# Shorter steps for the first attention, its head norms among the projections, and four smaller edits at the ends of stages

## The reference, cut to what matters

```
q = rms_norm(q.reshape(B, L, N_Q_HEADS, HEAD_DIM), q_norm_g)      # 8 heads of 64
k = rms_norm(k.reshape(B, L, N_KV_HEADS, HEAD_DIM), k_norm_g)     # 2 heads of 64
p = softmax(concatenate([s_band, s_meta, sink], axis=-1))         # window 128, block 128
out = p[band] @ v + p[meta] @ v_meta
...
mixed = concatenate([rms_norm(attn), rms_norm(ssm)]); h = h + mixed @ w_out
h = h + peer_ffn(rms_norm(h, norm2_g), ...)                       # 128 tiles of U, 128 of V
# second model, two layers:
x = x + 0.5 * swiglu(rmsnorm(x), w_gate, w_up, w_down)            # ffn1
x = x + (four mixers of rmsnorm(x)) @ w_out
x = x + 0.5 * swiglu(rmsnorm(x), w_gate, w_up, w_down)            # ffn2
```

## Time and profile before

| What | Value |
| --- | --- |
| median of 3 runs | 4655.22 us (4654.63 to 4656.16) |
| the profiled execution | 4656.73 us, span 4655.5 us |
| PE busy | 4155.0 us, 89% |
| DVE busy | 2403.9 us, 52% |
| ACT busy | 1352.5 us, 29% |
| POOL busy | 110.0 us, 2% |
| granted clock, mean | 0.922 |
| split on DVE (L343), mean of one | 1232 ns |
| projections of the first block end, first step of the merged part begins | 111.3 us |
| merged part ends, w_out begins | 373.6 us |

### The profile page before, as it was taken

The page is one execution under the profiler, slowest core; times in us unless marked ns, Lnnn a source line. Parts: engine busy times, 40 slices in busy tenths (PEclk is TensorE's granted clock), DMA queues, the critical chain, the costliest instruction groups (busy, mean ns, idle before and its releaser), DMA issues.

```text
span 4655.5 us, 46825 instructions
## 1 busy us (share of the span) xinstructions
PE 4155.0 (89%) x19069; PEld 3256.1 (70%) x19069; DVE 2403.9 (52%) x3798; ACT 1352.5 (29%) x2068; POOL 110.0 (2%) x210
## 2 busy tenths in 40 slices
PE   7468999999999999998998756899999987479999
PEld 6357887666678888877877535787778775357877
DVE  4834898777734444443323876433233249763331
ACT  3143322333333333323222222322132232223221
POOL 7000000000000000000000000000000000000000
PEclk9678999999999999999999776899999998768999
DMA  3002354555566666642332110123222221101231
GB/s 104 0 10 64 99 144 136 157 180 181 181 197 192 184 193 188 188 143 89 95 95 73 41 52 1 55 92 98 91 77 95 95 64 46 47 1 64 91 99 68
DMA packets 253334, 473.52 MB, mean 102 GB/s; under 512 B 15856, under 2 KB 138896, under 8 KB 250944
## 3 DMA queue, kind: packets, MB, share of 16 engines
q1 hardware_dynamic: 253120, 470.53, 33.1%
HBM read 399.95 MB, written 70.52 MB: 101 GB/s over the span
## 4 chain that ended last, share of the span: by engine, by line
PE 77%; DVE 17%; ACT 4%; issue 1%; DMA 0%; POOL 0%; DVEq 0%; ACTq 0%; POOLq 0%; SPq 0%
PE ps L352 23%; PE ps L353 22%; PE ps L354 22%; PE ps L455 2%; DVE arena L1792 2%; DVE arena L2642 1%; DVE st L2640 1%; PE ps L2191 1%; PE ps L2167 1%; DVE arena L2559 1%; DVE wtwo L343 1%; DVE arena L1108 1%; DVE arena L1788 1%; DVE arena L1789 1%; PE ps L1641 1%
## 5 line engine op out<-in xcount | busy, mean ns | idle before, releaser
L343 DVE TENSOR_TENSOR wtwo<-wraw,wtwo 128x1024 fp32r<-128x1024 f32 x414 | 508.5, 1232 | 832.4 <-ACT wtwo L333 832.1
L352 PE MATMUL ps<-XH,wtwo 128*128 128x512 f32 (+1 forms) x1936 | 794.5, 410 | 1.3 <-DVE XL L481 1.3
L353 PE MATMUL ps<-XL,wtwo 128*128 128x512 f32 (+1 forms) x1936 | 764.2, 395 | 0.0
L354 PE MATMUL ps<-XH,wtwo 128*128 128x512 f32 (+1 forms) x1936 | 761.2, 393 | 0.0
L333 ACT ACTIVATE wtwo<-wraw 128x1024 fp32r<-128x1024 f32 x414 | 435.5, 1056 | 447.0 <-PE ps L354 433.9
L343 DVE TENSOR_TENSOR wlast<-wraw,wlast 128x1024 fp32r<-128x1024 f32 x204 | 250.2, 1228 | 433.0 <-ACT wlast L333 432.9
L354 PEld LDWEIGHTS ps<-XH,wtwo 128*128 128x128 f32 x1936 | 365.6, 189 | 87.2
L352 PEld LDWEIGHTS ps<-XH,wtwo 128*128 128x128 f32 x1936 | 366.5, 189 | 74.6 <-issue 2.2
L353 PEld LDWEIGHTS ps<-XL,wtwo 128*128 128x128 f32 x1936 | 367.2, 190 | 70.9
L352 PE MATMUL ps<-XH,wlast 128*128 128x512 f32 x912 | 378.4, 415 | 4.5 <-DVE wlast L343 4.5
L354 PE MATMUL ps<-XH,wlast 128*128 128x512 f32 x912 | 362.4, 397 | 0.0
(11 more groups left out here) (445 smaller groups left out, 6742.1 us busy)
## 6 DMA issues: line engine op xcount, KB each, us to landing
wraw<-in_ut SPq DMA_DIRECT2D x128, 512.0 KB, 4.2
wraw<-in_v SPq DMA_DIRECT2D x128, 512.0 KB, 3.9
wraw<-in_ffn_gate SPq DMA_DIRECT2D x88, 512.0 KB, 3.5
wraw<-in_ffn_up SPq DMA_DIRECT2D x88, 512.0 KB, 3.5
wraw<-in_ffn_down SPq DMA_DIRECT2D x88, 512.0 KB, 3.6
acts<-arena SPq DMA_DIRECT2D x128, 256.0 KB, 4.5
gates<-arena SPq DMA_DIRECT2D x16, 2048.0 KB, 9.0
arena<-gates SPq DMA_DIRECT2D x32, 1024.0 KB, 8.1
```

The lines of the kernel that those rows point to most:

```text
L343: ve.e.tensor_tensor(W.items[n][8], W.rawof(n), W.items[n][7], ALU.subtract).then_inc(*ve.up("wlo", n))
L352: mm(out, lh, rh, start=start, stop=False)
L353: mm(out, lh, rl, start=False, stop=False)
L354: return mm(out, ll, rh, start=False, stop=stop)
```

## The change

Six edits:

1. **Units in four steps.** A unit's steps are now: scores of unit n + 1; turns of heads 0 and 1 and the value product of head 0; the rest of the turns and products; one step without PE work. ACT makes all four copies of a unit (L811), in the second and third step, and the exponentials of unit n + 1 come behind them, in the fourth. DVE makes no copies. The turned probabilities have one PSUM bank (3), the products another (4); before there were two banks for the turns and half of bank 2 for the products. The attention has 39 steps, the SSM still 60.
2. **Head norms among the projections.** DVE's work for q's heads stands behind the copies of q, and ACT's square root behind the splits for k and v; k's heads are done among the u projections.
3. **`xD` by token tile**: PE waits for each diagonal ahead of its matmul, in all eight norms.
4. **`ac_table`**: a square root of one column, put at the end of the attention's half of `ac_out`, ahead of the splits of `w_out` in both mixers, ahead of the splits of the down tiles in all four networks, and ahead of the first `ac_prep` of the V phase. It makes the compiler load the Sqrt table there.
5. **`TAIL` = 18**: the last four down tiles of each network are taken token tile by token tile, and DVE waits for each bank by itself. They form a group, so their places come back together.
6. **Waits** for `coef` and `masks` stand once, ahead of the units.

```diff
         for j in range(8):
             o = k.open(0, 8, "xT", n, j)
-            pe.wait_ge(*at("xD", n))
             for i in range(4):
+                pe.wait_ge(*at("xD", n, i))
...
+def ac_table(k):
+    k.ac.after().activation(k.ssq[:, 7:8], k.ones[:, 0:1], ACT.Sqrt).then_inc(*k.ac.up())
...
-        na, ns = 6 + 3 + 7 * 8 + 5 + 1 + 5, 60
+        na, ns = 3 + 8 * 4 + 4, 60
...
         splits(k, split_ac, "kv", 256)
+        self.ac_heads("q", 0, 32)
...
+        q = self.ve_heads(self.Q, "Q", 8, 4, 0, "q")
+        next(q)
         for c in range(2):
             split_ve(k, ("kv", c))
+        next(q)
...
+        kn = self.ve_heads(self.KV[:, :, 0:128], "KV", 2, 5, 40, "k")
         for m in range(4):
             split_ve(k, ("u", m))
+            if m < 2:
+                next(kn)
...
+            def turn(hq):
+                pe.wait_ge(*at("se", n))
+                o = k.open(3, 4, "pT", n, hq)
+                ...
+            def value(h):
+                pv = k.open(4, 5, "pv", n) if h == 0 else k.got("pv", n)
+                pe.wait_ge(*at("PT", n, h))
+                ...
+            yield
+            if n < 7:
+                scores(n + 1)
+            yield
+            turn(0)
+            turn(1)
+            value(0)
+            yield
+            turn(2)
+            value(1)
+            turn(3)
+            value(2)
+            value(3)
+            yield
...
         for n in range(8):
-            lo = 0 if n // 2 else 128
-            ...
+            yield
+            yield
+            turned(n, 0)
+            turned(n, 1)
+            yield
+            turned(n, 2)
+            turned(n, 3)
+            yield
             if n < 7:
-                yield from front(n + 1)
+                exps(n + 1)
...
     def ac_v(self):
         k, ac, at = self.k, self.k.ac, self.k.at
+        ac_table(k)
         for j in range(self.LEAD):
             self.ac_prep(j)
...
+        ws = {f: k.W.pair((*id, "down", f)) for f in range(self.TAIL, 22)}
+        for m in range(4):
+            for f, w in ws.items():
+                pe.wait_ge(*at("wlo", w[2]))
+                for n in range(2):
+                    last = one(f, m, n, w)
+                    if f == 21:
+                        last.then_inc(*pe.up("down", *id, "tile", m, n))
...
-        ve.wait_ge(*at("down", *id, 21))
         for m in range(4):
             for n in range(2):
+                ve.wait_ge(*at("down", *id, "tile", m, n))
```

More of the change, by code:

```diff
@@ L693, in ve_in, with ac_heads, ve_heads @@
         k.end("in", ve)
+    def ac_heads(self, name, base, n):
+        k, ac = self.k, self.k.ac
+        ac.wait_ge(*k.at(name + "var"))
+        ac.e.activation(k.st[:, base:base + n], k.st[:, base:base + n], ACT.Sqrt).then_inc(*ac.up(name + "sd"))
+    def ve_heads(self, x, event, nh, n, base, name):
+        k, ve, v, at = self.k, self.k.ve, self.k.ve.e, self.k.at
+        x = x.rearrange("p i (h e) -> p i h e", e=64)
+        t4 = self.tmp[:, 0:n * nh * 64].rearrange("p (i h e) -> p i h e", h=nh, e=64)
+        ss = k.st[:, base:base + n * nh]
+        for i in range(n):
+            ve.wait_ge(*at(event, i))
+        ve.after().tensor_tensor(t4, x, x, ALU.mult).then_inc(*ve.up())
+        ve.after().tensor_reduce(ss.rearrange("p (a b) -> p a b", b=nh), t4, AX, ALU.add).then_inc(*ve.up())
+        ve_rstd1(k, ss, 64).then_inc(*ve.up(name + "var"))
+        yield
+        ve.wait_ge(*at(name + "sd"))
+        v.reciprocal(ss, ss).then_inc(*ve.up())
+        ve.after().tensor_tensor(x, x, bc(ss.rearrange("p (a b) -> p a b", b=nh), 3, 64),
+                                 ALU.mult).then_inc(*ve.up(name + "n"))
+        yield
     def blocks(self, i):
@@ L713, in pe_att, with scores @@
         pe.e.transpose(o[:, 0:128], KV[:, 4, 0:128], k.ident[:, :]).then_inc(*pe.up("kT"))
-        yield
-        yield
-        def front(n):
+        def scores(n):
             i, hh = n // 2, n % 2
@@ L735, in front @@
                 last.then_inc(*pe.up(f"sm{r // 64}", n))
[L736 to L740, removed]
+        yield
+        scores(0)
         for n in range(8):
             i, hh = n // 2, n % 2
-            if n < 7:
-                yield from front(n + 1)
             vals = [None if kb == 0 and i == 0 else KV[:, (i - 1, i, 4)[kb], 128 + 64 * hh:192 + 64 * hh]
                     for kb in range(3)]
[L747 to L766, removed]
@@ L777, in ac_att, with exps @@
         a = ac.e.activation
+        st = k.st
         k.begin(ac, "in", "pe", "ac", "ve")
[L779 to L788, removed]
+        def exps(n):
             i = n // 2
@@ L798, in front, with turned @@
             last.then_inc(*ac.up("se", n))
-            yield
-        yield from front(0)
-        for n in range(8):
-            lo = 0 if n // 2 else 128
-            if n < 7:
[L805 to L815, removed]
+        def turned(n, hq):
+            lo = 0 if n // 2 else 128
+            ac.wait_ge(*at("pT", n, hq))
+            if 4 * n + hq >= 3:
+                ac.wait_ge(*at("pv", (4 * n + hq - 3) // 4, (4 * n + hq - 3) % 4))
+            a(self.PT[(4 * n + hq) % 3][:, lo:384], k.got("pT", n, hq)[:, lo:384],
+              ACT.Copy).then_inc(*ac.free(("pT", n, hq)))
+            ac.note("PT", n, hq)
+        yield
+        yield
+        exps(0)
+        for n in range(8):
+            yield
+            yield
+            turned(n, 0)
+            turned(n, 1)
+            yield
+            turned(n, 2)
+            turned(n, 3)
+            yield
+            if n < 7:
+                exps(n + 1)
+        yield
         ac.wait_ge(*at("ao", 7))
@@ L867, in ve_att, with largest @@
         last.then_inc(*ve.up())
-        yield
         sk = k.row("sink")
         ve.wait_ge(*at("rows"))
-        def front(n):
-            yield
+        ve.wait_ge(*at("masks"))
+        def largest(n):
             i, hh = n // 2, n % 2
@@ L883, in front @@
             ve.wait_ge(*at("sm1", n))
-            ve.wait_ge(*at("masks"))
             if n >= 2:
@@ L894, in front @@
             ve.after().tensor_scalar(mx, mx, -1.0, None, ALU.mult).then_inc(*ve.up("smx", n))
+        yield
+        largest(0)
+        for n in range(8):
+            i, hh = n // 2, n % 2
+            s0 = 64 + 16 * (n % 2)
+            den, es = st[:, s0 + 4:s0 + 8], st[:, s0 + 8:s0 + 12]
             yield
+            yield
+            if n < 7:
+                largest(n + 1)
             yield
@@ L1966, in plan_ffn @@
     for f in range(22):
-        k.W.add((name, l, "down", f), k.d[f"{name}_down{l}"][128 * f:128 * f + 128, :], 1, 1024)
+        k.W.add((name, l, "down", f), k.d[f"{name}_down{l}"][128 * f:128 * f + 128, :], 1, 1024,
+                group=(name, l, "tail") if f >= Ffn.TAIL else None)
 class Ffn:
+    TAIL = 18
     def __init__(self, k, name, l, gname, norm, last, before):
```

124 lines of the change are left out of this document (59 added, 65 removed).

## The result

The changed kernel takes 4577.72 us (median of four runs, 4575.17 to 4580.67) against 4655.69 us before (four runs, 4654.63 to 4657.46): a ratio of 0.9832, with a 95% interval from 0.9815 to 0.9849. That is 78 us less, where 70 were forecast. Its profiled execution took 4580.15 us, with a span of 4578.9 us against 4655.5; the mean granted clock rose from 0.922 to 0.929. Its four runs lie in two pairs, two near 4575.2 and two near 4580.4, and the profiled one is of the upper pair; so a difference of up to 3 us to the median is within their own spread.

The account below looks back on a forecast made before the run. PE carries 77% of the chain of waits; gains lie where it stands still, merged part and seams. 35 + 16.5 + 7.5 + 6.1 + 5 = 70 us less: 4585 us median; likeliest case 4572 to 4600, overall range 4562 to 4612.

Parts of the forecast that it names:

- (a): Merged part's start: moving head norms among the projections saves 11.3 us, less 0.5 for slowing POOL (at most 3).
- (b): Merged part's first stretch, to the SSM's 17th step: 3.5 units instead of 1.3 make it 21 us longer (13 to 30).
- (c): DVE's long stretch of 14 steps: 3.5 units instead of 2, fewer copies, 5 us longer (3 to 10).
- (d): The y stretch, 76.1 us: three units and the Exp/Gelu switches leave, 22 us less (12 to 32).
- (e): GLU to the SSM's end, 42.1 us: scores, a value product and exponentials with their table load leave, some 5 us less.
- (h): Diagonals: PE starts behind the first of four, 0.94 us less in each of eight norms, 7.5 us.
- (f): End of the merged part: the 23.4 us in which only the attention's rest runs go whole.
- (g): Down tiles: 4.1 us less behind three networks, 4.2 at the fourth; 16.5 us in sum (13 to 17).
- (i): Tables: six norms lose their load, 7.7 us less; the V phase adds 1.6 us; net 6.1 us.
- (j): Clock: shorter waits give 1 us in each of six norms, V's start may lose 1; net 5 us less.
- the first rival: Merged part gives only the head norms back: it gains 15 us, the change 50, giving 4605 us; chance 0.17.
- everything overlaps better: Clock stays high and y stretch falls: 46 us from merged part, 16 clock, 30 rest, giving 4563 us; chance 0.12.

Follow-up runs that it names:

- e7: Changed kernel with the V phase's table fetch moved from ahead of its first tile to behind its ninth: 4576.58 us, ratio 0.9830 to before.
- e6: Changed kernel with POOL's scratch and the head norms' scratch exchanged, so q's scalings overwrite nothing POOL reads: 4572.43 us, ratio 0.9820 to before.
- e1: Kernel before with only the last four down tiles of each network taken token tile by token tile: 4641.29 us, ratio 0.9964.
- e4: Kernel before with only the merged part's edits (units in four steps, copies on ACT, head norms among the projections): 4610.83 us, ratio 0.9898.
- e2: Kernel before with only one event for each of a norm's four diagonals: 4650.64 us, ratio 0.9987.
- e3: Kernel before with only the square root's table fetched early in four places: 4659.65 us, ratio 1.0003.
- e10: Changed kernel without the four early table fetches: 4587.68 us, ratio 0.9853 to before.
- e8: Changed kernel with two banks in turn for the turned probabilities, values' products back in the scores' third bank: 4578.14 us, ratio 0.9836 to before.
- e5: Changed kernel with the head norms of q and k back at the beginning of the merged part: 4586.95 us, ratio 0.9852 to before.
- e9: Kernel before with all seam edits together (down tiles, diagonals, tables), merged part as it was: 4626.11 us, ratio 0.9936.
- e11: Changed kernel with both the exchanged scratch of e6 and the later V table fetch of e7: 4573.18 us, ratio 0.9824 to before.
- e12: e11 plus 24 identity products filling PE's wait ahead of each norm but the first: 4579.55 us, ratio 0.9837 to the kernel before.

## Why the prediction was right, and where its terms were off

The time and its direction came as forecast, within the likeliest case's own range. The terms, in their order:

(a) Wrong in its small part, right in its large one. The head norms' 11.3 us went, but POOL's slowing cost 2.9 to 4.5 us of wait (e7's and the changed kernel's rows) instead of 0.5. A single split beside POOL was the wrong row to size it by. The sum of DVE's two-operand operations, 6.4 us, was the right measure, and my upper bound of 3 us was too low. e6 took this loss away.

(b), (c), (d), (e) The stretches last 54.5, 74.1, 52.1 and 35.3 us, forecast 57, 75, 54 and 37. Each was a little shorter, and the part started 3.1 us earlier, of which (h) had only 0.94; e1, which changes nothing ahead of it, starts it 2.4 us earlier too, so some 2 us are the spread of the projections. The merged part's term was therefore too small: 35 forecast, 41.7 in the profiled execution, 45.6 in e4, whose y stretch had the higher clock. The mechanism is the one named: units in PE's idle time, copies no longer behind long operations (PE's wait ahead of the value products, 67.5 us, is 11.7), and the 23.4 us of (f) gone whole. No run takes the four steps and the copies on ACT apart, so their shares are argued from the rows.

(g) 16.5 forecast, 15.2 in e1. The waits fell to 5.4 us there (5.6 expected). With (h) and (i) the waits ahead of norms 1 to 7 should have lost 26.6 us, and lost 27.7.

(h) 7.5 forecast, 5.8 in e2: of 0.94 us less wait a norm keeps part, as the half clock then reaches further into its matmuls (4.5 us of wait leave 2.5 us lost in norm 7, 5.4 us left 2.1).

(i) Its mechanism held: no load in seven of the eight norms, a load of 1.28 us at the V phase. Its size can't be told by itself: −3 in e3, +10 in e10. By the Trainium skill ("ScalarE: Activation LUTs", What ACT_TABLE_LOAD costs) a switch has a drain of 1.38 us beside its 1.28; the V phase's wait grew by 1.52, the load and the root of 0.20. ACT's Gelu ends there 0.02 us ahead of the load and the root starts 0.01 us behind it, so no run here shows the drain.

(j) Near in its sum, 6.0 for 5, and wrong in both halves, which offset one another. Six norms (1 and 3 to 7) lost 14.9 us to the clock before and 6.3 after, 8.6 gained for 6 assumed. V's start lost 2.6 for 1 assumed.

With the forecast's own waits for (g), (h) and (i), and the rest from the profiled executions, the sum is 41.7 + 16.5 + 6.6 (h, without the first norm, which the 41.7 hold) + 7.7 − 1.5 + 8.6 − 2.6 = 77.0, and the spans differ by 76.6. That the terms add up so well is in part luck: the seams' 30.1 us of (g), (h) and (i) gave 17.8 as single edits, and nothing in the forecast says that the second blocks' attention loses its clock with one of them and keeps it with all.

Of the signs, the first scaling (115.8), the waits of 3.2 us (3.4 expected) and 3.54 us (3.6) and the norms without a load came as named; the end of L1344 (L1374 now) came at 331.9 and w_out's first matmul at 333.3, earlier than the 336 to 341 and 340 that were given. One sum of the forecast is wrong: with all bounds at their ends the merged part gives 9 to 56 us and not 15 to 50, and the first rival, by the bounds that it names, 11 and not 15. The forecast itself doesn't hang on it.

Of the rivals, "everything overlaps better" was nearer than its chance of 0.12 said for the merged part (46 us there, 45.6 in e4), and wrong for the norms, of which only two kept 2.4 GHz. The one bank was a wait of 4.4 us that moves elsewhere if taken away (e8).

e6 is the fastest kernel of the study, 4572.4 us, 0.9820 of the kernel before.

## What to carry to other kernels

Where PE waits a few microseconds at many seams, the edits that shorten one wait can be worth more together than alone (29.7 us for 17.8 here): measure them together as well as one by one, and expect each alone to read several microseconds off, by a clock that falls in stages that the edit doesn't touch. Work moved from a stage's start beside another engine's chain is free only if that engine isn't slowed past its own deadline: sum the operations that contend, and look who reads the result first. And when a repair shows its own mechanism in the trace but not in the time, compare the later stages that it doesn't touch, stage by stage, before calling it worthless.

## What the runs showed of the hardware that was not expected

The granted clock falls or stays after one and the same wait. At 3.1 us ahead of norm 1 it stayed at 1.00 in the changed kernel, e5, e8 and e10, and fell to 0.50 in e2, e6, e7, e9 and e11 (1.5 to 3.1 us lost). At 2.26 to 2.37 us ahead of the last down products it stayed at 1.00 in eleven of the fourteen traces and fell in e2, e3 and e12 (1.7 us). At the V phase's 2.02 us it stayed in the kernel before, e1, e4, e7 and e11, and fell in e2, e10 and e12 (1.7 us); with 3.54 us there it fell in all six traces (1.7 to 2.7 us). Between the changed kernel and e7 a shift of some microseconds is all that lies ahead of such a place. By the Trainium skill ("TensorE: Matmul & The Clock Gate", What's actually happening) the chip's watch on TensorE runs free of the kernel's start; that fits, but what decides in a single place was not settled here.
